# Expert choice by a one-hot matmul in place of a second tournament, and the tokens' split ahead of the weights'

## The reference, cut to what matters

```python
def expert_choice_ffn(h, w_router, w_gate, w_up, w_down):
    t = h.reshape(bsz * seq, d)                 # d = 1024
    cap = CAPACITY_FACTOR * n_tok // N_EXPERTS  # 64 and 32
    probs = jax.nn.softmax(t @ w_router, axis=-1)
    aff, idx = lax.top_k(probs.T, cap)
    xe = t[idx]
    hid = jax.nn.silu(einsum("ecd,edf->ecf", xe, w_gate)) * einsum("ecd,edf->ecf", xe, w_up)
    ye = einsum("ecf,efd->ecd", hid, w_down) * aff[..., None]
    out = jnp.zeros_like(t).at[idx.reshape(-1)].add(ye.reshape(-1, d))
```

## Time and profile before

| | |
|---|---|
| median of 3 runs | 2879.83 us (2878.42 to 2884.75) |
| the profiled execution, its own time | 2879.83 us |
| its span, first to last instruction | 2878.0 us |
| TensorE busy (share of the span) | 2635.4 us (92%) |
| VectorE busy | 2087.3 us (73%) |
| ScalarE busy | 1583.4 us (55%) |
| GpSimd busy | 364.9 us (13%) |
| mean granted clock of TensorE | 0.958 of full speed |

### The profile page before, as it was taken

One profiled execution on the slowest core, in us unless ns is written; L12 is line 12 of the kernel. 1 busy time (PEld: TensorE's weight loads), 2 busy tenths in 40 slices (PEclk: granted clock), 3 DMA queues, 4 the chain that ended last, 5 costly groups with the idle time before them and its releaser, 6 DMA issues. The chain is left out here.

```text
span 2878.0 us, 34293 instructions
## 1 busy us (share of the span) xinstructions
PE 2635.4 (92%) x13487; PEld 2064.1 (72%) x13487; DVE 2087.3 (73%) x2122; ACT 1583.4 (55%) x1926; POOL 364.9 (13%) x473
## 2 busy tenths in 40 slices
PE   3799999999998769884999999999999999999995
PEld 3689888988887658773777666767677676766763
DVE  3465676477556333328999999999999999999995
ACT  2245354535434231214777777777777777777774
POOL 0033123303325100000000000000000000000000
PEclk9899999999998789997999999999999999999997
DMA  2222222223233254327999999999999999999994
GB/s 95 86 71 85 98 96 79 94 85 105 83 107 112 90 186 140 135 104 288 374 373 378 378 371 380 370 384 370 376 378 377 373 380 373 379 375 371 376 372 180
DMA packets 71487, 707.01 MB, mean 246 GB/s; under 512 B 9392, under 2 KB 14128, under 8 KB 48672
## 3 DMA queue, kind: packets, MB, share of 16 engines
q1 hardware_dynamic: 47296, 628.95, 56.3%
q0 software_dynamic: 14208, 56.73, 6.2%
q10 hardware_dynamic: 9824, 19.14, 1.7%
HBM read 669.94 MB, written 34.85 MB: 245 GB/s over the span
## 5 line engine op out<-in xcount | busy, mean ns | idle before, releaser
L1876 DVE TENSOR_TENSOR wl<-raw,wh 128x2048 fp32r<-128x2048 f32 x528 | 1194.1, 2290 | 117.4 <-ACT wh L1815 106.9
L1815 ACT ACTIVATE wh<-raw 128x2048 fp32r<-128x2048 f32 x528 | 990.8, 1911 | 258.4 <-PE p_y L1965 224.9
L1938 PE MATMUL p_gu<-wh,xh 128*96 128x512 f32 x1408 | 566.5, 402 | 3.0 <-DVE xl L1882 3.0
L1938 PE MATMUL p_gu<-wh,xl 128*96 128x512 f32 x1408 | 555.5, 395 | 0.0
L1938 PE MATMUL p_gu<-wl,xh 128*96 128x512 f32 x1408 | 553.5, 393 | 0.0
L860 PE MATMUL pp<-h_hi,wx_hi 128*128 128x256 f32 (+1 forms) x896 | 325.9, 364 | 15.2 <-DVE wx_lo L1079 15.2
L860 PE MATMUL pp<-h_lo,wx_hi 128*128 128x256 f32 (+1 forms) x896 | 310.2, 346 | 0.0
L860 PE MATMUL pp<-h_hi,wx_lo 128*128 128x256 f32 (+1 forms) x896 | 309.6, 346 | 0.0
L1938 PEld LDWEIGHTS p_gu<-wl,xh 128*96 128x96 f32 x1408 | 227.4, 162 | 100.3
L1938 PEld LDWEIGHTS p_gu<-wh,xh 128*96 128x96 f32 x1408 | 227.6, 162 | 91.5 <-DVE wl L1876 4.4
L1938 PEld LDWEIGHTS p_gu<-wh,xl 128*96 128x96 f32 x1408 | 227.6, 162 | 83.3
(11 more groups left out here) (240 smaller groups left out, 3754.1 us busy)
## 6 DMA issues: line engine op xcount, KB each, us to landing
raw<-in_w_e SPq DMA_DIRECT2D x176, 3072.0 KB, 10.9
dec<-acs POOLq DMA_DIRECT2D x48, 512.0 KB, 4.8
w_raw<-in_w_x SPq DMA_DIRECT2D x48, 512.0 KB, 3.5
w_raw<-in_w_g SPq DMA_DIRECT2D x24, 512.0 KB, 3.4
gx<-fo ACTq DMA_DIRECT2D x24, 384.0 KB, 2.3
g_tab<-gx POOLq DMA_DIRECT2D x8, 1152.0 KB, 6.6
...
```

Source lines behind the costliest of these rows:

```text
L1815: act.activation(wh[:, n % 2, at:at + hi - lo], raw[:, n % RAW, lo:hi], ACT.Copy).then_inc(s_wh, 1)
L1876: dve.tensor_tensor(wl[:, n % 2, to], raw[:, n % RAW, lo:hi], wh[:, n % 2, to].bitcast(F32), ALU.subtract).then_inc(s_wl, 1)
L1938: mm = pe.matmul(p_gu[n % 2][0:SLOTS, 0:w], xx[:, side, k * SLOTS:(k + 1) * SLOTS], ww[:, n % 2, k * w:(k + 1) * w], start=(k == 0 and i = ...
```

## The change

Marks become token numbers in another way. A scan over `gt` gives each picked token its place among the picks of its expert (1 to 64 or 32), zero for the others. TensorE turns the places round (`posT`, token by row), and VectorE compares them with the numbers 1 to 64 (`slot1`), which gives for every tile of tokens and every expert a one-hot table, token x place (`oh_p`, `oh_s`). TensorE multiplies these tables with `pairs`, two columns for each token and expert: the token's number and its probability. So one set of matmuls gives `idx` and the probabilities `aff` of all experts. Two small tables, `slot1` (64 numbers, to all 128 partitions) and `tokid`, take the place of `tids`, and VectorE waits for both at the start of its list.

As `aff` is known from `choose`, `h2` keeps 1,024 columns and the transfer of `prob` into it is dropped; GpSimd's `affinity` is gone, and ScalarE copies the expert's column of `aff` to `aff_c` ahead of scaling the result. `idx` has 17 columns instead of 16, the last a copy of the first. In `experts`, ScalarE and VectorE split the first tokens before they split the first weight unit.

```diff
--- before.py
+++ after.py
@@ -1493,7 +1493,7 @@
                 sp.wait_ge(s_h, t + 1)
-                sp.dma_start(h2[t * P:(t + 1) * P, 0:D], hh[:, t % 2, :]).then_inc(s_h2[t % 2], 16)
+                sp.dma_start(h2[t * P:(t + 1) * P, :], hh[:, t % 2, :]).then_inc(s_h2[t % 2], 16)
             for s in s_xa + s_h2:
...
@@ -1613,7 +1613,7 @@
-def choose(nc, A, cst, prob, raw, s_raw, idx, h2):
+def choose(nc, A, cst, prob, raw, s_raw, idx, aff):
...
@@ -1626,22 +1626,26 @@
         gt, eq, rank, one = (a.sb(n, [ROWS, SEQS[0]]) for n in ("gt", "eq", "rank", "one"))
-        tids = a.sb("tids", [ROWS, SEQS[0]])
-        picks = a.sb("picks", [ROWS, CAPS[0]])
+        posT = a.sb("posT", [P, NTP, ROWS])
+        slot1 = a.sb("slot1", [P, CAPS[0]])
+        tokid = a.sb("tokid", [P, NT])
+        oh_p = a.sb("oh_p", [P, NTP, E, CAPS[0]])
+        oh_s = a.sb("oh_s", [P, NT - NTP, E, CAPS[1]])
+        pairs = a.sb("pairs", [P, NT, E, 2])
         p_s = a.ps("c_ps", [P, 512])
+        p_t = a.ps("c_pt_", [P, 512])
         p_l = a.ps("c_pl", [P, 512])
-        m_c, m_pr, s_c, s_pb, s_pt, s_ch, s_picks, s_ia, s_init = a.sems(
-            "c_m", "c_pr", "c_c", "c_pb", "c_pt", "c_ch", "c_picks", "c_ia", "c_init")
+        m_c, s_c, s_pb, s_pt, s_ch, s_pos, s_posT, s_oh, s_ia, s_init = a.sems(
+            "c_m", "c_c", "c_pb", "c_pt", "c_ch", "c_pos", "c_posT", "c_oh", "c_ia", "c_init")
...
         def _(sp):
-            sp.dma_start(tids[:], A["tids"]).then_inc(m_c, 16)
-            sp.dma_start(h2[:, D:D + E].rearrange("(c p) e -> p c e", p=P), prob[:]).then_inc(m_pr, 16)
+            sp.dma_start(slot1[:], A["slot1"].partition_broadcast(P)).then_inc(m_c, 16)
+            sp.dma_start(tokid[:], A["tokid"]).then_inc(m_c, 16)
             for u in range(RAW):
                 load_unit(sp, A, raw, s_raw, 0, u)
-            sp.wait_ge(m_pr, 16)
...
@@ -1649,10 +1653,19 @@
             mm.then_inc(s_pt, 1)
-            pe.wait_ge(s_picks, 1)
-            pe.transpose(p_l[0:CAPS[0], 0:E], picks[0:E, :], ident[0:E, 0:E])
-            pe.matmul(p_l[CAPS[0]:SLOTS, 0:E], picks[32:ROWS, 0:CAPS[1]], ident[32:ROWS, 32:ROWS],
-                      start=True, stop=True).then_inc(s_ia, 1)
+            pe.wait_ge(s_pos, 1)
+            for b in range(NTP):
+                mm = pe.transpose(p_t[:, b * ROWS:(b + 1) * ROWS], rank[:, b * P:(b + 1) * P], ident[0:ROWS, 0:ROWS])
+            mm.then_inc(s_posT, 1)
+            pe.wait_ge(s_oh, 1)
+            for e in range(E):
+                for b in range(NTP):
+                    pe.matmul(p_l[0:CAPS[0], 2 * e:2 * e + 2], oh_p[:, b, e, :], pairs[:, b, e, :],
+                              start=(b == 0), stop=(b == NTP - 1))
+                for b in range(NT - NTP):
+                    mm = pe.matmul(p_l[CAPS[0]:SLOTS, 2 * e:2 * e + 2], oh_s[:, b, e, :], pairs[:, NTP + b, e, :],
+                                   start=(b == 0), stop=(b == NT - NTP - 1))
+            mm.then_inc(s_ia, 1)
...
@@ -1666,9 +1679,12 @@
             ch = Steps(dve, s_ch)
+            dve.wait_ge(m_c, 32)
             dve.wait_ge(s_init, 2)
...
             dve.tensor_copy(pblk[:, 0:NT - NTP, 32:ROWS], prob[:, NTP:NT, :]).then_inc(s_pb, 1)
+            dve.tensor_copy(pairs[:, :, :, 0], tokid[:].unsqueeze(2).to_broadcast([P, NT, E]))
+            dve.tensor_copy(pairs[:, :, :, 1], prob[:])
             dve.wait_ge(s_pt, 1)
...
@@ -1688,20 +1704,26 @@
-            dve.wait_ge(m_c, 16)
-            ch(dve.tensor_tensor(work[:], gt[:], tids[:], ALU.mult))
-            for r in range(CAPS[0] // 8):
-                ins = dve.max(picks[:, 8 * r:8 * r + 8], work[:])
-                if r < CAPS[0] // 8 - 1:
-                    ch(ins)
-                    ch(dve.match_replace(work[:], picks[:, 8 * r:8 * r + 8], work[:], -2.0))
-            ins.then_inc(s_picks, 1)
+            ch(dve.tensor_tensor_scan(work[:], one[:], gt[:], 0.0, ALU.mult, ALU.add))
+            dve.tensor_tensor(rank[:], work[:], gt[:], ALU.mult).then_inc(s_pos, 1)
+            dve.wait_ge(s_posT, 1)
+            ch(dve.tensor_copy(posT[:].rearrange("p b r -> p (b r)"), p_t[:, 0:NTP * ROWS]))
+            for b in range(NTP):
+                dve.tensor_tensor(oh_p[:, b], posT[:, b, 0:E].unsqueeze(2).to_broadcast([P, E, CAPS[0]]),
+                                  slot1[:].unsqueeze(1).to_broadcast([P, E, CAPS[0]]), ALU.is_equal)
+            for b in range(NT - NTP):
+                ins = dve.tensor_tensor(oh_s[:, b], posT[:, b, 32:ROWS].unsqueeze(2).to_broadcast([P, E, CAPS[1]]),
+                                        slot1[:, 0:CAPS[1]].unsqueeze(1).to_broadcast([P, E, CAPS[1]]), ALU.is_equal)
+            ins.then_inc(s_oh, 1)
             dve.wait_ge(s_ia, 1)
-            dve.tensor_copy(idx[:], p_l[0:SLOTS, 0:E]).then_inc(s_c, 1)
+            got = p_l[0:SLOTS, 0:2 * E].rearrange("p (e k) -> p e k", k=2)
+            dve.tensor_copy(idx[:, 0:E], got[:, :, 0])
+            dve.tensor_copy(idx[:, E:E + 1], got[:, 0:1, 0])
+            dve.tensor_copy(aff[:], got[:, :, 1]).then_inc(s_c, 1)
             dve.wait_ge(s_c, 1)
...
-def experts(nc, A, cst, raw, s_raw, h2, xa, idx):
+def experts(nc, A, cst, raw, s_raw, h2, xa, idx, aff):
...
@@ -1710,8 +1732,8 @@
         idx_s = a.sb("idx_s", [SLOTS, 1], I32)
-        aff = a.sb("aff", [SLOTS, E])
-        xe = a.sb("xe", [SLOTS, D + E])
+        aff_c = a.sb("aff_c", [SLOTS, 1])
+        xe = a.sb("xe", [SLOTS, D])
         xh = a.sb("xh", [P, 2, KD * SLOTS], F32R)
...
@@ -1772,12 +1794,6 @@
-            def affinity(e):
-
-                pool.wait_ge(s_xt, e + 1)
-                pool.tensor_copy(aff[:, e:e + 1], xe[:, D + e:D + e + 1]).then_inc(s_aff, 1)
-                pool.wait_ge(s_aff, e + 1)
-
             def scatter(e):
...
@@ -1791,15 +1807,15 @@
             gather(0)
-            affinity(0)
+            pool.wait_ge(s_xt, 1)
             gather(1)
             for e in range(E - 2):
-                affinity(e + 1)
+                pool.wait_ge(s_xt, e + 2)
                 gather(e + 2)
                 scatter(e)
-            affinity(E - 1)
             scatter(E - 2)
             scatter(E - 1)
+            pool.wait_ge(s_g, 16 * E)
...
@@ -1822,10 +1838,11 @@
                 act.wait_ge(s_ye, e + 1)
+                act.activation(aff_c[:], aff[:, e:e + 1], ACT.Copy).then_inc(s_aff, 1)
                 act.wait_ge(s_aff, e + 1)
...
                 act.wait_ge(s_free, e + 1)
-                act.activation(ye[:], p_y[0:SLOTS, :], ACT.Copy, scale=aff[:, e:e + 1]).then_inc(s_ye, 1)
+                act.activation(ye[:], p_y[0:SLOTS, :], ACT.Copy, scale=aff_c[:]).then_inc(s_ye, 1)
...
@@ -1858,9 +1875,9 @@
             act.sem_inc(s_wh, W0)
+            tokens(0, 0)
             for k in range(3):
                 high(0, 0, k)
-            tokens(0, 0)
             unit(0, 0, following(0, 0))
...
@@ -2057,13 +2074,14 @@
     gx = nc.dram_tensor("gx", (KD, 3, P, T), F32).ap()
-    h2 = nc.dram_tensor("h2", (T, D + E), F32).ap()
+    h2 = nc.dram_tensor("h2", (T, D), F32).ap()
     xa = nc.dram_tensor("xa", (T, D), F32).ap()
...
         cst = [a.sb(n, [P, P]) for n in ("ident", "tri_f", "tri_b", "ones")] + [a.sb("neg_half", [P, NT])]
-        idx = a.sb("idx", [SLOTS, E], I32)
+        idx = a.sb("idx", [SLOTS, E + 1], I32)
+        aff = a.sb("aff", [SLOTS, E])
         prob = a.sb("prob", [P, NT, E])
...
@@ -2080,8 +2098,8 @@
             s_raw = l.sems(*[f"e_raw{i}" for i in range(RAW)])
-            choose(nc, A, cst, prob, raw, s_raw, idx, h2)
-            experts(nc, A, cst, raw, s_raw, h2, xa, idx)
+            choose(nc, A, cst, prob, raw, s_raw, idx, aff)
+            experts(nc, A, cst, raw, s_raw, h2, xa, idx, aff)
         final(nc, A, cst, xa, outs)
...
@@ -2136,9 +2154,6 @@
         edge[q, half:win - 1] = win / (win - 1 - np.arange(half - 1))
-    tids = np.zeros((32 + E, SEQS[0]), np.float32)
-    tids[0:E] = np.arange(SEQS[0])
-    tids[32:, 0:SEQS[1]] = np.arange(SEQS[0], T)
     arrays = {
...
@@ -2166,7 +2181,8 @@
         "edge": edge.reshape(-1),
-        "tids": tids,
+        "slot1": np.arange(1, CAPS[0] + 1, dtype=np.float32),
+        "tokid": np.arange(T, dtype=np.float32).reshape(NT, P).T,
     }
...
```

## The result

The changed kernel takes 2905.55 us (median of 4 runs, 2901.87 to 2909.09) beside 2881.66 for the kernel before (4 runs): a ratio of 1.0089, 95% interval [1.0077, 1.0101]. It is slower by 0.9%. The profiled execution took 2905.18 us, its span 2903.4, so the span is 25.4 us longer than the 2878.0 before. 19.5 were predicted, and the range ended at 2906.0. The median of these 4 runs lies at its upper edge, and that of all 21 executions of the changed kernel on record, 2907.49 us (2901.58 to 2910.78), lies 1.5 us beyond it. Neither got there by a case that had set that edge. The 66 executions of the kernel before have a median of 2883.25, so over all executions the change costs 24.2 us.

The account below looks back on a forecast made before the run. The prediction took TensorE to bound the experts and one serial chain to bound `choose`. Its terms 14.3 + 3.2 + 2.0 = 19.5 us on 2879.8 gave 2899.3 us, range 2889.5 to 2906.

Parts of the forecast that it names:

- a case that had set that edge: Upper end of the range, 2906: narrow loads with a minimum cost and late weight loads together, with some of their overlap.
- burst: In `choose`, 96 small f32 matmuls (192 load and matmul pairs) at clock 0.50: 17.4 us, bounds 8.6 and 21.5.
- wait for the constants: Head of VectorE's list in `choose`: start at 1295.7 instead of 1292.46, +3.2 us, lower bound +1.9.
- six comparisons: VectorE in `choose`, making the one-hot tables: four of 1,024 columns and two of 512, 5.9 us with the gap.
- `choose` behind `gt`, net of 12.61: Serial chain in `choose`: 26.9 us added, less the removed second tournament's 12.61, +14.3 us.
- first tokens ahead of the first unit: Start of `experts`: the first gate_up starts 2.0 us later with no further loss, bounds 1.5 and 3.
- half price: Rival on the small matmuls in `choose`: 8.6 us instead of 17.1, total 2890.8; chance 0.13.
- a floor per pair: Rival on the small matmuls in `choose`: narrow loads cost 0.112 each, 21.5 us, total 2903.7; chance 0.09.
- The clock: Sign in `choose`: the granted clock stays at 0.50 through the 192 weight loads; a rise would make the prediction wrong.
- The loads: Rival at the start of the experts: the fourth unit's transfer 7.4 us later paces the stage, total 2904.7; chance 0.05.
- The experts' pace: Predicted unchanged near 94 us an expert; rival: faster matmuls from moved tiles or quieter GpSimd, equal or faster, chance 0.07.
- the wait that was to absorb it: ScalarE's 174 waits for TensorE, 224.9 us in sum, hide its extra activation; uncovered it would cost 3 us.

Follow-up runs that it names:

- the ruler: Changed kernel with rows of 16 f32 products, 128 to 16 stationary columns wide, added behind the 96 small matmuls: 0.212 to 0.030 us a pair of load and matmul.
- two runs: Changed kernel with all small matmuls of the prompt first, then all of the sample: 17.36 us for them instead of 20.16; single run 2905.34 us.
- a forced start: Changed kernel with five unused f32 matmuls of 512 columns ahead of the small ones: clock 1.00 for five experts, then 0.50; single run 2910.43 us.
- the pair of versions that differ only in it: The pipelined version against the same with the broadcasts `bias` and `alog` issued first: 2884.19 and 2880.80 us, ratios 1.0005 and 0.9992.
- the pipelined version: Changed kernel with old split order, late constants wait, bf16 tables, each tile's products issued after its comparison, one change of output partitions: 2884.19 us, ratio 1.0005.

## Why the prediction was wrong: what held and what failed

The direction, the place and the mechanism were right: a serial stage got longer by the burst, nothing hid it, and the experts' pace didn't move. The size was wrong. The sum was 19.5 and the span grew by 25.4, so it was 5.9 short, and over all executions 4.7 short. The step that failed is the burst: 17.4 us in the sum, 20.16 measured. The rest of the gap are stretches that the sum put at nothing, less 1.0 us that the wait for the constants had too much. By its own steps:

| step | predicted | measured |
|---|---|---|
| scan, masking | 1.25, 0.73 | 1.25, 0.74 |
| transposes | 0.85 | 0.69 |
| copy of `posT` | 0.39 | 0.40 |
| six comparisons | 5.9 | 5.88 |
| burst | 17.4 | 20.16 |
| three copies | 0.4 | 0.3 |
| `choose` behind `gt`, net of 12.61 | +14.3 | +16.8 |
| wait for the constants | +3.2 | +2.2 |
| first tokens ahead of the first unit | +2.0 | +2.1 |
| longer at the lower clock behind it | 0 | +1.0 |
| stages ahead of `choose` | 0 | +2.5 |
| gather, experts, stages behind | 0 | +0.8 |

- **The burst, mis-sized by 2.8 us.** "I take the cost as proportional to the stationary columns: 0.107 for 64, 0.053 for 32" holds: the ruler gives 0.105 and 0.053, and the burst in two runs took 17.36 us. What the step left out is that the listing of products alternates between tiles of 64 and of 32 columns. 30 changes more, at 0.093, are the 2.8. The nearest row, L1514, has one width throughout, so it could not show the price; the order of the loops in the code could have raised the question. Both rivals fell: half price needs the higher clock, which even a forced start didn't keep, and a floor per pair would have shown in the narrow rows of the ruler.
- **The clock.** That the burst stays at 0.50 was right, as the window from 1324.50 to 1344.30 shows. But the first `gate_up` starts at the lower clock too, and stays there 4.8 us where it was 3.0 (1333.83 to 1336.87) before. At the lower clock its matmuls follow each other every 0.43 us, at the higher every 0.23, so 1.8 us more of it costs 0.8 of the +1.0. The prediction had no term for it, but it isn't shown to come from the change: it is 6.1 in the kernel before with nothing but shifted tiles, 4.3 in the changed kernel with the order or the constants undone, 3.9 with two runs. The pair of traces at hand happened to have 3.0 and 4.8.
- **The constants, 1.0 too much.** The step took `edge`'s 4.2 us for a transfer that spreads 64 numbers over 128 partitions. Here `slot` took 2.4 and `tokid`, issued 0.39 later, 2.7, and it is `tokid` that VectorE waited for. The measured value lies near the step's lower bound, 1.9, and partly by luck: that bound put 0.7 us between the two issues and 2.2 for the second transfer, where 0.39 and 2.7 were measured. The same shape at another place had been a bad proxy. Undoing it gave the 2.2 back.
- **The first tokens ahead: right**, 2.06 us beside 2.0 in the trace, 2.4 to the end in both pairs of kernels that were alike but for it.
- **The stages ahead: put at nothing.** The prediction compared only the stages that the change touches. In the two traces `choose` starts 2.5 us later, and VectorE's wait for `alog` is 3.1 us longer at its place. The 2.5 is one pair of executions, and the start of `choose` spreads over 11.5 us in the profiles; over all executions the medians differ by 24.2 us, of which 22.9 lie behind the block's start in the traces, so 1.3 is the better estimate (it takes the 22.9 from one pair of traces). That the late `alog` is behind it is supported, not proved, by the pair of versions that differ only in it, 3.4 us apart; why it is late isn't shown. It came in every kernel here whose SBUF tiles or inputs differ from those of the kernel before, unless `alog` was issued first, and in neither of the two that share them (in the one with only the order changed `alog` landed after 11.8 us).
- **The loads: right that they don't pace the stage.** TensorE has no such wait behind the start, and the expert's interval is unchanged.
- **The experts' pace: right.** 93.91 beside 93.90. ScalarE's extra activation, 0.18 us for each expert, did no harm to it; the wait that was to absorb it shows no trace of it, 226.9 us beside 224.9.

On the weight load the Trainium skill ("TensorE: Matmul & The Clock Gate", section "LDWEIGHTS (loading the stationary operand)") says P / 1.2 ns. For 64 columns that is 53 ns. The bf16 loads of the pipelined version take 58 at the lower clock, so there the rule fits; the f32 loads of the ruler take 105, twice that. The prediction's 8.5 us by the rule had already counted two loads for an f32 product, so this factor of two is what stood between it and the 17.1 from the rows. Together the two make an f32 product four times a bf16 one.

For the comparisons the Trainium skill ("VectorE: DVE Perf Modes", section "The perf-mode tier table (the rule you actually need)") gives `tensor_tensor` twice the pace when it works on bf16 in SBUF. The trace agrees roughly: four comparisons take 4.63 us with f32 operands, 2.50 with all three in bf16, 1.85 times the pace.
